# First norm of a hybrid decoder step: the norm's 1/rms applied behind the projections instead of ahead of them

## What is computed

```python
def rmsnorm(x, g):
    return x * lax.rsqrt(jnp.mean(x * x, axis=-1, keepdims=True) + EPS) * g

def mixer(h, ...):                      # h = rmsnorm(x, norm_mix_g)
    proj = jnp.einsum('btd,de->bte', h, w_in)
    bg, cg, hc, q, k, v, g = jnp.split(proj, cuts, axis=-1)
    u = cg * hc
    full = jnp.concatenate([conv_buf, u], axis=1)
    conv_out = sum([full[:, j:j + t] * conv_w[j] for j in range(CONV_K)])
    y_conv = bg * conv_out
    qh, kh = rotary(q, pos), rotary(k, pos) * HD ** -0.5
    o, s_new = retention(qh, kh, v, ret_state)
    o = groupnorm(o) * ret_gn_g + ret_gn_b
    y = jnp.concatenate([y_conv, silu(g) * o], axis=-1)
    return jnp.einsum('bte,ed->btd', y, w_out), full[:, t:], s_new
...
x = x + mixer(rmsnorm(x, norm_mix_g))
x = x + peer(rmsnorm(x, norm_ffn_g))    # top-16 of 16384 experts, done densely
return rmsnorm(x, norm_final_g)
```

## Time and profile before

| | us |
|---|---|
| median of 3 runs | 2276.17 (2275.16 to 2276.96) |
| the profiled execution | 2276.12 |
| its span | 2274.6 |
| TensorE busy in the span | 2212.3 (97%) |
| VectorE busy | 1462.3 (64%) |
| ScalarE busy | 878.3 (39%) |
| DMA moved | 379.38 MB, 167 GB/s |

### The profile page before, as it was taken

One profiled execution on the slowest core, in us unless ns is written; L12 is line 12 of the kernel. 1 busy time (PEld: TensorE's weight loads), 2 busy tenths in 40 slices (PEclk: granted clock), 3 DMA queues, 4 the chain that ended last, 5 costly groups with the idle time before them and its releaser, 6 DMA issues.

```text
span 2274.6 us, 51127 instructions
## 1 busy us (share of the span) xinstructions
PE 2212.3 (97%) x20233; PEld 2170.1 (95%) x20233; DVE 1462.3 (64%) x2730; ACT 878.3 (39%) x1171; POOL 33.5 (1%) x55
## 2 busy tenths in 40 slices
PE   4999999998999999999999999999999999999997
PEld 3999989997999999999999999999999999999997
DVE  4576766546778856666565666666666587765554
ACT  2444433332343433333433434333343433334433
POOL 0000000000000000000000000000000000000000
PEclk8999989998999999999999999999999999999998
DMA  3555535553445555445545555545454555455553
GB/s 137 187 179 175 170 122 181 189 187 111 149 158 186 179 182 168 162 155 167 181 169 176 168 175 169 172 168 171 167 167 167 178 166 165 162 168 184 177 174 105
DMA packets 104167, 379.38 MB, mean 167 GB/s; under 512 B 12192, under 2 KB 12464, under 8 KB 103760
## 3 DMA queue, kind: packets, MB, share of 16 engines
q1 hardware_dynamic: 100368, 365.28, 48.4%
q0 software_dynamic: 3648, 11.87, 1.8%
HBM read 370.06 MB, written 6.96 MB: 166 GB/s over the span
## 4 chain that ended last, share of the span: by engine, by line
PE 85%; DVE 2%; ACT 0%; issue 0%; DVEq 0%; ACTq 0%
PE bank L705 27%; PE bank L706 26%; PE bank L707 26%; PE bank L872 4%; PE bank L835 1%; DVE pair L1013 0%; DVE stats L996 0%; PE bank L818 0%; DVE acc L1553 0%; PE bank L729 0%; DVE xlo L1020 0%; DVE xhi L1018 0%; PE bank L763 0%; DVE stats L1004 0%; DVE stats L1000 0%
## 5 line engine op out<-in xcount | busy, mean ns | idle before, releaser
L705 PE MATMUL bank<-xhi,whi 128*128 128x264 f32 x4224 | 1219.1, 289 | 20.2 <-DVE xlo L1020 20.0
L979 DVE TENSOR_TENSOR wlo<-raw,whi 128x1024 fp32r<-128x1024 f32 x688 | 828.3, 1222 | 629.7 <-ACT whi L494 627.8
L706 PE MATMUL bank<-xlo,whi 128*128 128x264 f32 x4224 | 1202.7, 285 | 0.0
L707 PE MATMUL bank<-xhi,wlo 128*128 128x264 f32 x4224 | 1202.1, 285 | 0.0
L494 ACT CAST whi<-raw 128x1024 fp32r<-128x1024 f32 x688 | 706.9, 1048 | 757.9 <-PE bank L707 739.2
L705 PEld LDWEIGHTS bank<-xhi,whi 128*128 128x128 f32 x4224 | 800.7, 190 | 34.8 <-issue 24.7
L706 PEld LDWEIGHTS bank<-xlo,whi 128*128 128x128 f32 x4224 | 802.1, 190 | 0.5
L707 PEld LDWEIGHTS bank<-xhi,wlo 128*128 128x128 f32 x4224 | 797.9, 189 | 0.0
L705 PE MATMUL bank<-wexp_hi,whi 128*128 128x264 f32 x1024 | 293.0, 286 | 0.0
L707 PE MATMUL bank<-wexp_hi,wlo 128*128 128x264 f32 x1024 | 290.5, 284 | 0.0
L706 PE MATMUL bank<-wexp_lo,whi 128*128 128x264 f32 x1024 | 290.0, 283 | 0.0
(11 more groups left out here) (189 smaller groups left out, 1073.0 us busy)
## 6 DMA issues: line engine op xcount, KB each, us to landing
raw<-halves SPq DMA_DIRECT2D x688, 512.0 KB, 3.3
s_old<-ret_state POOLq DMA_DIRECT2D x8, 512.0 KB, 6.1
ret_sample<-s_new POOLq DMA_DIRECT2D x8, 512.0 KB, 4.0
acc<-xT SPq DMA_DIRECT2D x4, 528.0 KB, 11.1
yT<-acc SPq DMA_DIRECT2D x4, 528.0 KB, 2.6
tables<-shape_constants POOLq DMA_DIRECT2D x1, 1584.0 KB, 8.7
hid<-keysT POOLq DMA_DIRECT2D x1, 1024.0 KB, 5.6
ret_prompt<-state POOLq DMA_DIRECT2D x8, 64.0 KB, 2.6
```

The lines of the kernel that those rows point to most:

```text
L705: nc.tensor.matmul(out, whi[:, s, c], mh[c], start=start and c == 0, stop=False)
L706: nc.tensor.matmul(out, whi[:, s, c], ml[c], start=False, stop=False)
L707: mm = nc.tensor.matmul(out, wlo[:, s, c], mh[c], start=False, stop=stop and c == HALF - 1)
L979: v.tensor_tensor(wlo[:, s], raw[:, s], whi[:, s].bitcast(F32), ALU.subtract).then_inc(lo_done, 1)
```

## The change

The first norm's 1/rms is no longer applied to x. ScalarE writes `xhi` as x times gain when a block of x has landed, VectorE makes `xlo` in one operation, and the first tile works on that. The squares are summed by TensorE between the blocks of the second tile, and 1/rms (`rx`) is made behind that. It is multiplied into the four rotation tables (cosq, sinq, cosk, sink, 4 x 264 columns), into `vT` and the gate as VectorE takes them from PSUM, and as `rx2` = rx squared into the convolution's `hcs` (for the product of two tiles), with one more product by `rx` for the third tile. The loads are issued in another order: SyncE takes the gain first and mixes x blocks with weight halves, and GpSimd waits for the last x block ahead of all its loads.

```diff
@@ -406,11 +412,22 @@
         def _(sp):
+            def x_block(c):
+                sp.dma_start(acc[:, 4 * c:4 * c + 4, :], xT[:, 4 * c:4 * c + 4, :]).then_inc(x_in[c], 16)
...
+            sp.dma_start(gains[:, 0, :], norm_mix).then_inc(gain_in, 16)
+            x_block(0)
+            first_half(0)
+            x_block(1)
+            x_block(2)
+            first_half(1)
+            x_block(3)
+            first_half(2)
             sp.dma_start(keep[:], consts[:, 0:KEEP]).then_inc(keep_in, 16)
-            for c in range(4):
-                sp.dma_start(acc[:, 4 * c:4 * c + 4, :], xT[:, 4 * c:4 * c + 4, :]).then_inc(x_in[c], 16)
-            for s in range(RING):
-                sp.dma_start(raw[:, s], halves[s]).then_inc(raw_full[s], 16)
+            first_half(3)
@@ -445,8 +462,9 @@
         def _(pool):
+            pool.wait_ge(x_in[3], 16)
             pool.dma_start(tables[:], consts[:, KEEP:NCONST]).then_inc(consts_in, 16)
-            for i, g in enumerate((norm_mix, norm_ffn, norm_fin)):
+            for i, g in ((1, norm_ffn), (2, norm_fin)):
@@ -517,20 +535,37 @@
-            hi_half(0, 0)
-            hi_half(0, 1)
+            act.wait_ge(gain_in, 16)
             for c in range(CH):
                 if c % 4 == 0:
                     act.wait_ge(x_in[c // 4], 16)
-                squares_of(c, c, acc[:, c, :])
-            root(1)
+                nc.scalar.activation(xhi[:, c, :], acc[:, c, :], ACT.Identity, scale=gains[:, 0, c:c + 1])\
+                    .then_inc(xh_ready, 1)
+                if c == 3:
+                    hi_half(0, 0)
+                if c == 11:
+                    hi_half(0, 1)
+
+            def first_squares():
+                hi_half(0, 2)
+                hi_half(0, 3)
+                for c in range(CH):
+                    squares_of(c, c, acc[:, c, :])
+                    if c == HALF - 1:
+                        hi_half(0, 4)
+                hi_half(0, 5)
+                root(1)
...
-                if tiles:
-                    tile_done(r, 0)
-                    nc.scalar.copy(vT[:], bank[0][:, 0:T]).then_inc(bank_free[0], 1)
+                if tiles and not first:
                     ahead(r, 1)
...
-                    if norm:
-                        act.wait_ge(y_ready, h - 1)
-                    nc.scalar.activation(silu[:], bank[3][:, 0:T], ACT.Silu).then_inc(bank_free[3], 1)
+                    act.wait_ge(bank_free[3], h)
+                    nc.scalar.activation(silu[:], silu[:], ACT.Silu).then_inc(silu_done, 1)
@@ -580,10 +612,6 @@
-                        if n == 0:
-                            tile_done(r0 + i * 6, k)
-                            act.wait_ge(y_ready, HEADS + i * 4 + j)
-                            nc.scalar.copy(hcs[:], bank[k % BANKS][:, 0:T]).then_inc(bank_free[k % BANKS], 1)
@@ -733,10 +765,6 @@
-            pe.wait_ge(keep_in, 16)
-            for c in range(CH):
-                add_squares(c, c)
@@ -787,10 +815,15 @@
                 for k, part in enumerate((turn, states, outputs, mean)):
+                    beside = (None, None)
+                    if first and k == 1:
+                        pe.wait_ge(keep_in, 16)
+                        beside = tuple(lambda c, s=s: add_squares(s * HALF + c, s * HALF + c) for s in range(2))
                     if att:
                         part(h - 1)
                     if tiles:
-                        tile(r, k, h, k, xhi, xlo, norm_waits(0) if first and k == 0 else ({}, {}))
+                        tile(r, k, h, k, xhi, xlo, norm_waits(0) if first and k == 0 else ({}, {}), beside=beside)
@@ -1020,14 +1053,28 @@
-            dve.wait_ge(consts_in, 16 * CONST_LOADS)
...
-            normalise(0)
+            for c in range(CH):
+                dve.wait_ge(xh_ready, c + 1)
+                ins = v.scalar_tensor_tensor(out=xlo[:, c, :], in0=acc[:, c, :], scalar=gains[:, 0, c:c + 1],
+                                             in1=xhi[:, c, :].bitcast(F32), op0=ALU.mult, op1=ALU.subtract)
+                if c % 2:
+                    ins.then_inc(norm_ready, 1)
+                if c == 3:
+                    lo_half(0, 0)
+                if c == 11:
+                    lo_half(0, 1)
+
+            def first_norm():
+                mean_square(1.0 / D, EPS, bank[7][:, 0:T], [(sq_used, CH)])
+                ahead(0, 2)
+                reciprocal_root(1, rx[:])
+                dve.wait_ge(consts_in, 16 * CONST_LOADS)
+                at = CONSTS["cosq"][0] - KEEP
+                four = tables[:, at:at + 4 * T].rearrange("p (n t) -> p n t", n=4)
+                ch.did(v.tensor_tensor(four, four, rx[:].unsqueeze(1).to_broadcast([P, 4, T]), ALU.mult))
+                ch.did(v.tensor_tensor(rx2[:], rx[:], rx[:], ALU.mult))
+                ch.wait()
@@ -1087,27 +1134,43 @@
-                dve.wait_ge(bank_free[3], p + 1)
+                dve.wait_ge(silu_done, p + 1)
...
+            def values_out(r):
+                tile_done(r, 0)
+                v.tensor_tensor(vT[:], bank[0][:, 0:T], rx[:], ALU.mult).then_inc(bank_free[0], 1)
+
+            def gates_out(p):
+                dve.wait_ge(half_used, RING * (p * 2) + 2 * BANKS)
+                v.tensor_tensor(silu[:], bank[3][:, 0:T], rx[:], ALU.mult).then_inc(bank_free[3], 1)
...
                 if tiles:
                     ahead(r, 0)
+                if first:
+                    ahead(r, 1)
+                    first_norm()
+                    values_out(r)
...
-                if tiles:
+                if tiles and not first:
+                    values_out(r)
                     ahead(r, 1)
...
                     normed(h - 2)
+                if att:
+                    gates_out(h - 1)
                 if tiles:
-                    ahead(r, 2)
+                    if not first:
+                        ahead(r, 2)
...
+                    tile_done(r, 3 * j)
+                    v.tensor_tensor(hcs[:], bank[bh][:, 0:T], rx2[:], ALU.mult).then_inc(bank_free[bh], 1)
                     tile_done(r, 3 * j + 1)
...
                     dve.wait_ge(bank_free[bb], o4 + (3 * j + 2) // BANKS + 1)
+                    ch.did(v.tensor_tensor(yv[:], yv[:], rx[:], ALU.mult))
                     split_y(HEADS + c)
```

39 lines of the change are left out of this document (23 added, 16 removed).

## The result

The changed kernel takes **2254.88 us** (median of 4 runs, 2254.45 to 2256.79), the kernel before 2275.9 beside it; the ratio is 0.991, with a 95% interval of 0.9899 to 0.9924. 2254.2 was predicted. The profiled execution took 2255.14 us, its span is 2253.6.

The account below looks back on a forecast made before the run. TensorE, 85% of the span, was taken as the bound, so only its idle or half-clock time pays. 2276.12 - 24.5 (start) + 2.2 (clock) + 0.4 (heads) = 2254.2 us, range 2250.5 to 2260.5.

Parts of the forecast that it names:

- The loads: At the start: with the tables behind x, the first block lands at 4.8, 1.40 of it data at 385 GB/s.
- The first tile: First projection tile: TensorE starts at 10.1, runs at half clock for 4.5 us and ends the tile at 18.0.
- The squares: Second tile: the squares lie in TensorE's stream, 0.445 us each, 7.1 for 16, so the tile takes 12.9.
- S: The end of the squares in TensorE's second tile, forecast at 31.0 us.
- Behind the squares: From the squares' end to `turn(0)`: casts, splits, reciprocal and rotations take 18.6 us, leaving TensorE a wait of 7.0.
- The clock behind the wait: At `turn(0)` and the tile behind it: half clock after the wait costs 2.2 us, between 0 and 4.5.
- The heads: Head without tiles: the gate product on the path costs 0.4 us, bounds 0 and 1.0; nothing while tiles cover.
- (a): Ahead of `turn(0)`: the rotation keeps up, no wait, the clock holds; 31.5 us gained, 2245.0; chance 0.06.
- (b): At the start: x blocks land no earlier, everything up to S shifts by 3 to 6 us, 2258 to 2260; chance 0.12.
- (c): First tile: too many gaps for the clock, which stays low into the second tile; 2261 to 2268; chance 0.08.
- (d): Heads and convolution chunks: VectorE becomes the bound, slower than before, 2281 and more; chance 0.02.
- (e): ScalarE's table load: an unseen drain adds 1.3 us ahead of the first split and the root; 2256.8; chance 0.03.

Follow-up runs that it names:

- e8_short_squares: Changed kernel with twelve of the first norm's sixteen square sums taken over 128 of 264 columns; median 2254.76 us.
- e1_fast: Changed kernel, chain behind the squares reordered: casts between squares, reciprocal before half 7's split, query swapped into its own buffer; 2247.61 us, ratio 0.9873.
- e2_fill: Changed kernel with 52 matmuls that nobody reads put into the wait ahead of `turn(0)`; median 2254.24 us.
- e6_table_early: Changed kernel with one ScalarE operation more ahead of the wait for x, so that its table is loaded there; median 2255.43 us.
- e5_dose_conv: Changed kernel with eight unread VectorE products (2.85 us) ahead of the split in each of the convolution's eight chunks; 2259.8 us.
- e4_after_oldloads: Changed kernel with the earlier kernel's order of loads, gain still first, without GpSimd's wait for the last block; 2264.13 us, ratio 0.9955.
- the doses: Changed kernel with eight unread VectorE products ahead of each head's value product (2260.17 us) or of the split in each convolution chunk (2259.8 us).
- the two `early` kernels: e6_table_early, 2255.43 us, and e1_fast with the same ScalarE operation added ahead of the wait for x, 2245.99 us.
- e10_warm: e1_fast plus the ScalarE operation ahead of the wait for x and ten unread matmuls ahead of the first tile; 2248.73 us, ratio 0.988.

## Why the prediction was right, point by point

**The loads.** The first block landed at 6.03, not 4.8. The issue was where I had it, but from it to the landing 4.6 us passed instead of 3.4. What was off is the data's part of the term, 1.40 us: the sum had 385 GB/s from the start, and for the block alone. The windows (as above, with DMA share and GB/s at the end) show less at first:

```profile
2.00:3.00 1.00, 0.00 (x0) 0.00 (x0) 0.00 (x0) 0.00 (x0) 0.00 (x0) 1.00 1.03 92
3.00:4.00 1.00, 0.00 (x0) 0.00 (x0) 0.00 (x0) 0.00 (x0) 0.00 (x0) 1.00 0.55 194
```

That is 0.29 MB in 2 us, 1.25 us short of the rate. From 4 to 6 the rate was 364 and 386, and by 6.0 some 1.04 MB had moved, of which the block is 0.54, so the weight half queued behind it was already being served. Which of the two made the block late isn't separated. The page of DMA issues, KB each and us to landing:

```profile
acc<-xT SPq DMA_DIRECT2D x4, 528.0 KB, 6.8
```

6.8 for 11.1 before. The order of the landings was right, so the whole start only slid by 1.2 us: first matmul at 11.30 for 10.1.

**The first tile.** It began at half clock, as the slow weight loads had said, though its windows print 1.00. The half clock lasted 5.7 us for 4.5, which costs 0.6 us more. The tile ended at 19.8 for 18.0.

**The squares.** 0.81 us apart in the second tile, which took 13.0 us for 12.9; `e8_short_squares` shows that they are on the path. S came at 32.85 for 31.0, all but 0.1 of it inherited from the start and the first tile.

**Behind the squares.** From S to `turn(0)` 18.55 us for 18.6 (18.5 by its own terms, 13.1 + 5.37), with 6.79 of wait for 7.0. The parts were somewhat further off than the sum: the reciprocal started at S + 6.2 (6.3), the key was rotated at S + 12.9 (13.1). `e1_fast` shows that the chain is what sets it.

**The clock behind the wait.** 8.47 less 6.90 is 1.57 for the 2.2 foreseen; `e2_fill` measures it by itself, 1.55. The mechanism was right, and the size goes by where the clock falls: 1.57 here, 2.65 in `e6_table_early` (9.55 less 6.90), 2.5 in `e5_dose_conv`.

**The heads.** The gate product stands in the last head as foreseen. From VectorE's reciprocal there (275.71) to the square that it waits for, ScalarE's `gnorm`, it takes 6.44 us for 6.09 before: 0.35, for 0.4 predicted.

```profile
281.35 0.42 DVE L1147 TENSOR_TENSOR silu<-bank,rx 128x264 f32<-128x264 f32 x1
281.69 0.42 DVE L1124 SCALAR_TENSOR_TENSOR dev<-bank,oT 128x264 f32<-128x264 f32 x1
```

```profile
281.81 0.42 ACT L591 ACTIVATE silu<-silu 128x264 f32<-128x264 f32 x1 [0.68 <-DVE silu L1147]
282.15 0.42 ACT L599 ACTIVATE gnorm<-dev 128x264 f32<-128x264 f32 x1
```

The whole way from `states(0)`, at equal clock stretches of 17.1 us, grew from 223.8 to 224.6, so the heads cost some 0.8; the other 0.4 isn't located. In the profiled run of the changed kernel it was hidden by the short stretch.

**The convolution.** Nothing, as taken: from the last head's reciprocal to the second norm's it takes 242.9 us before and after. And `e5_dose_conv` shows how much more there would have been room for.

**The sum.** 22.7 gained for 24.5 (start 1.2, first tile's clock 0.6), 1.6 for 2.2 lost behind it. From `states(0)` to the convolution the profiled run gave 1.0 back, by its clock. From the last head's reciprocal to the final norm's it took 1.1 more. On this way, at the second norm, the clock came back at 539.4, fell again at 542.8 and returned at 553.0, where the kernel before had one low stretch, until 572.7; that this is the 1.1 isn't shown, since the same way differs by up to 1.4 us between kernels that don't touch it. 2202.2 from `turn(0)` to the end of the span for 2203.1. So 2254.2 for 2254.9 owes something to luck: the start was taken 1.8 us too early, and what lies behind it 0.9 us too dear, and this partly cancels. The first tile's clock alone could have moved the start by 1.3.

**The rivals.** (a) is a kernel that can be written, `e1_fast`, but not this one; that the order could give only 1 or 2 us was wrong. (b) did not happen: the first block landed at 6.03 and the last by 12.6. As a kernel it is `e4_after_oldloads`: 2264.1, more than the 2258 to 2260 that I gave it, since the weights come late as well. (c) did not happen; the squares' tile ran at full clock. (d) is excluded by the doses. (e), a drain behind the table load: "ScalarE: Activation LUTs" of the Trainium skill, section "What ACT_TABLE_LOAD costs", has 2.66 us with it. The changed kernel's first `xhi` starts 1.29 us behind the load's start (6.03 to 7.32), and in the two `early` kernels that time is gone; the trace decides for 1.3.

## What to carry to other kernels

A norm's scale that is constant along the contraction can be applied behind the matmul, and then the product may start on the first block of its input; the loads are to be reordered with it. Here either half paid alone, 7.8 and 13.7 us of 22.7 at the first fixed point behind them. What is left behind the statistics is a chain through two in-order queues, and there the order of the items decides: 7 us lay in moving a few casts and splits around the squares, the reciprocal and the rotations, and in one more buffer for the query's swap. When a change wins a few microseconds, compare milestones between two fixed instructions in the traces and list the low-clock stretches: here they alone gave or took 1 to 2 us at each of three places.

## What the runs showed of the hardware

- In these traces a low-clock stretch came in two lengths at a place, for nearly the same work: 13.7 or 17.1 us in the last head, 6.8 or 10.2 us at `turn(0)`. The fall came 2.2 to 5.2 us after TensorE had gone idle ahead of `turn(0)` (42.19 to 44.4 in `e6`, 44.61 to 47.8 in the changed kernel, 41.73 to 45.8 in `e8`, 43.33 to 48.5 in `e5_dose_conv`). So the same wait left between 3.3 and 5.7 us of the stretch to the work behind it, at a cost of 1.6 to 2.65 us.
- The printed clock is 1.00 ahead of TensorE's first work and all through it, in all traces of the new order; the matmuls, 0.22 us apart and then 0.12, say that it was the lower level: 0.22 is also their pace in the first tile of the kernel before, where the windows print 0.50. With work from 1.58 us on (`e10_warm`) the first tile ran at the upper one.
- Behind one wait of 2.15 us, after a millisecond of dense work, the clock fell for 3.4 us (`e10_warm`): with a second gap of 0.36 the pause cost 4.4, twice its length.
- The time from issue to landing of a small load depends on what is queued: 192 KB took 2.5 us as the first of its queue and 8.8 behind the four x blocks and three weight halves.
